# The second block's output product as seven half-size products (Strassen's scheme) instead of eight, with VectorE forming the sums before and after

## What is computed

```python
merged = (jax.nn.sigmoid(g_diff) * (o_diff @ w_proj_diff[layer])
          + jax.nn.sigmoid(g_mla) * (o_mla @ w_proj_mla[layer]))
x = x + merged @ w_out[layer]
...
return rms_norm(x, norm_final)
```

## Time and profile before

| | |
|---|---|
| time, median of 3 | 1087.87 us (1087.51 to 1088.33) |
| the profiled execution: span from its first to its last instruction | 1085.8 us; its time outside the span is not recorded, the median of the timed ones is 2.1 us above it |
| TensorE busy | 1072.4 us (99%) |
| weight loads | 860.1 us (79%) |
| VectorE busy | 712.5 us (66%) |
| ScalarE busy | 420.2 us (39%) |
| mean granted TensorE clock | 0.999 of full speed |

### The profile page before, as it was taken

The page is one execution under the profiler, slowest core; times in us unless marked ns, Lnnn a source line. Parts: engine busy times, 40 slices in busy tenths (PEclk is TensorE's granted clock), DMA queues, the critical chain, the costliest instruction groups (busy, mean ns, idle before and its releaser), DMA issues.

```text
span 1085.8 us, 13595 instructions
## 1 busy us (share of the span) xinstructions
PE 1072.4 (99%) x5395; PEld 860.1 (79%) x5397; DVE 712.5 (66%) x1149; ACT 420.2 (39%) x661; POOL 0.2 (0%) x4
## 2 busy tenths in 40 slices
PE   9999999999999999999999999999999999999998
PEld 6777877977878888888888887887776777888886
DVE  6998877868678887854588745654568446464441
ACT  6513655334443223222222234744367443323232
POOL 0000000000000000000000000000000000000000
PEclk9999999999999999999999999999999999999999
DMA  8422122221213323234322234323121222033302
GB/s 279 126 78 79 47 71 79 71 86 39 79 60 106 117 79 105 59 89 129 122 78 88 65 94 143 98 97 117 44 78 40 78 78 78 1 116 117 102 35 78
DMA packets 100239, 95.59 MB, mean 88 GB/s; under 512 B 5952, under 2 KB 91216, under 8 KB 100176
## 3 DMA queue, kind: packets, MB, share of 16 engines
q1 hardware_dynamic: 100000, 94.71, 27.9%
q10 hardware_dynamic: 176, 0.02, 0.0%
HBM read 92.60 MB, written 2.10 MB: 87 GB/s over the span
## 4 chain that ended last, share of the span: by engine, by line
PE 91%; DVE 5%; ACT 2%; issue 1%; DMA 1%; SPq 0%; DVEq 0%; ACTq 0%
PE ring L1036 22%; PE ring L1038 22%; PE ring L1037 22%; PE bank L1036 3%; PE bank L1038 3%; PE bank L1037 3%; PE bank L1500 1%; PE bank L1295 1%; DVE w_lo L1929 1%; PE bank L1267 1%; DMA w_raw<-in_w_in 1%; PE bank L1200 1%; PE bank L1280 1%; PE bank L1524 1%; PE bank L1473 1%
## 5 line engine op out<-in xcount | busy, mean ns | idle before, releaser
L1036 PE MATMUL ring<-act_hi,w_hi 128*128 128x512 f32 (+2 forms) x808 | 320.2, 396 | 0.9 <-DVE xT L2312 0.5
L1038 PE MATMUL ring<-act_hi,w_lo 128*128 128x512 f32 (+2 forms) x808 | 313.5, 388 | 0.0
L1037 PE MATMUL ring<-act_lo,w_hi 128*128 128x512 f32 (+2 forms) x808 | 313.2, 388 | 0.0
L1588 ACT ACTIVATE w_hi<-w_raw 128x2048 fp32r<-128x2048 f32 (+5 forms) x96 | 159.8, 1665 | 249.7 <-PE ring L1038 200.6
L1929 DVE TENSOR_TENSOR w_lo<-w_raw,w_hi 128x2048 fp32r<-128x2048 f32 (+4 forms) x101 | 190.3, 1886 | 4.2 <-ACT w_hi L1588 3.9
L1036 PEld LDWEIGHTS ring<-act_hi,w_hi 128*128 128x128 f32 x808 | 151.8, 188 | 37.1 <-issue 3.9
L1038 PEld LDWEIGHTS ring<-act_hi,w_lo 128*128 128x128 f32 x808 | 151.7, 188 | 31.6
L1037 PEld LDWEIGHTS ring<-act_lo,w_hi 128*128 128x128 f32 x808 | 151.8, 188 | 31.3 <-issue 1.9
L1036 PE MATMUL ring<-hidH,w_hi 128*128 128x512 f32 x176 | 68.5, 389 | 0.0
L1037 PE MATMUL ring<-hidL,w_hi 128*128 128x512 f32 x176 | 68.5, 389 | 0.0
L1038 PE MATMUL ring<-hidH,w_lo 128*128 128x512 f32 x176 | 68.5, 389 | 0.0
(11 more groups left out here) (363 smaller groups left out, 1618.9 us busy)
## 6 DMA issues: line engine op xcount, KB each, us to landing
w_raw<-in_w_in SPq DMA_DIRECT2D x30, 1024.0 KB, 5.3
w_raw<-in_w_up SPq DMA_DIRECT2D x22, 1024.0 KB, 5.1
w_raw<-in_w_out SPq DMA_DIRECT2D x8, 1024.0 KB, 5.1
w_raw<-in_w_down SPq DMA_DIRECT2D x8, 768.0 KB, 4.7
w_raw<-in_w_down SPq DMA_DIRECT2D x8, 640.0 KB, 4.3
w_raw<-in_w_in SPq DMA_DIRECT2D x7, 512.0 KB, 4.7
xin<-in_xt SPq DMA_DIRECT2D x8, 256.0 KB, 4.1
xT<-in_xt SPq DMA_DIRECT2D x2, 1024.0 KB, 6.6
```

The lines of the kernel that those rows point to most:

```text
L1036: pe.matmul(out, ah, bh, start=(first and n == 0), stop=False)
L1037: pe.matmul(out, ah, bl, start=False, stop=False)
L1038: mm = pe.matmul(out, al, bh, start=False, stop=(last and n == len(pairs) - 1))
L1588: return act.activation(out, src, func, **more)
```

## The change

The 512 x 1024 by 1024 x 1024 product is cut into 2 x 2 quarters: token halves by depth halves on the left, depth halves by column halves on the right (B11, B12, B21, B22, one weight slot each). Eight quarter products become seven, `prod` 0 to 6, each over two blocks of 128 tokens (t = 0, 1). Four of them take a sum on the left (S1 to S4, 128 x 1024), four a sum on the right (T1 to T4, 128 x 2048); these are formed by VectorE in float32 (`s_sum`, `t_sum`) and then split into high and low parts like any operand (`s_split`, `split_form`). `snap`, `s17`, `u_sum`, `v_sum` and `c_sum` put the products together in `xo` in SBUF, with one addition of a bank each (`snap` is a copy by ACT). The residual is opened into products 2, 5 and 6 and, for one quarter, into two tiles of the ring (`res`). Products 1, 3, 4, 5 use T3 with S3, T2 with S2, T1 with S1, B22 with S4; product 6 uses T4 with `mH`. The order of stages is again by hand. `merged` is now kept in float32 (`mt2`, eight slices) for the S sums. B22 and B21 are loaded into the space of the block's input, so only after tile `gm7`. Squares for the norm are taken from `xo` (`sq_early`), scaling of the first finished half rows is `scaled`, of the other `final`. Several semaphores are merged to make room, which moves nothing.

```diff
--- before.py
+++ after.py
+        mt2 = [sb(f"mt2{i}", [P, 4, T], F32, M + (108, 90)[i]) for i in range(2)]
+
+        b22 = sb("b22", [P, SLOT], F32, 64)
+        b21 = sb("b21", [P, SLOT], F32, 72)
+        t1 = sb("t1", [P, SLOT], F32, 80)
+        Sf = {n: sb(f"S{n}f", [P, 4, 256], F32, M + at) for n, at in ((3, 22), (1, 98), (2, 102), (4, 16))}
...
+        B11 = len(chunks)
+        chunk("B11", k_out2[:, 0:4, 0:512])
+        for name in ("T3", "B21", "T2", "T1", "B22", "T4"):
+            form(name)
+        PROD = ("B11", "T3", "B21", "T2", "T1", "B22", "T4")
...
+            if c == 3:
+                stage("s_split", 3)
+                stage("t_sum", "T1")
             for kind in ("pd", "pm"):
                 for i in (2 * c, 2 * c + 1):
+                    if (kind, i) == ("pm", 6):
+                        stage("t_sum", "T3")
                     in_tile(kind, i, f"pj{c}")
+                    if (kind, i) == ("pm", 6):
+                        split_form("T3")
+            if c == 1:
+                stage("s_sum", 3)
+
+        both("prod", 0)
         stage("m_flush")
-        for half in range(2):
-            for part in range(2):
-                chunk(f"w_out2{half}{part}", k_out2[:, 4 * part:4 * part + 4, 512 * half:512 * half + 512])
-            for b in range(NB):
-                stage("out_a", half, b)
-            for b in range(NB):
-                tile(("out", half, b), f"w_out2{half}1")
-                stage("out", half, b)
-                if half == 1:
-                    stage("final", b)
-            last_use[chunk_of[f"w_out2{half}0"]] = tile_at["out", half, 0]
+        split_form("B21")
+        stage("t_sum", "T2")
+        both("snap")
+        both("prod", 1)
+        stage("s_sum", 1)
+        stage("s_sum", 2)
+        split_form("T2")
+        stage("s_split", 2)
+        both("s17")
+        for t in range(2):
+            tile(("res", t))
+            stage("res", t)
+        both("prod", 2)
+        stage("c_sum", 2, 0)
+        stage("s_split", 1)
+        stage("c_sum", 2, 1)
+        split_form("T1")
+        stage("s_sum", 4)
+        each("sq_early", 0, 1)
+        both("prod", 3)
+        split_form("B22")
+        stage("s_split", 4)
+        both("u_sum")
+        both("prod", 4)
+        stage("t_sum", "T4")
+        split_form("T4")
+        both("c_sum", 4)
+        both("v_sum")
+        each("sq_early", 2, 3)
+        both("prod", 5)
+        for t in range(2):
+            stage("scaled", t)
+            stage("c_sum", 5, t)
+        each("final", 0, 1)
+        each("scaled", 2, 3)
+        both("prod", 6)
+        for t in range(2):
+            stage("c_sum", 6, t)
+            stage("final", 2 + t)
...
+            wait_split(sp, B11 - 1)
+            quarter_in(raw[(B11 + 1) % 2], 0, 1, raw_in[(B11 + 1) % 2])
+            sp.wait_ge(tile_done, upto(("gm", KD - 1)))
+            quarter_in(b22, 1, 1, block_in[0])
+            quarter_in(b21, 1, 0, block_in[1])
...
+                elif kind == "prod":
+                    n, t = s[1:]
+                    at = slice(P * t, P * t + P)
...
+                    elif n == 6:
+                        pe.wait_ge(part_sum, 2 * t + 4)
+                    to = bank[2 * (n % 3) + t]
+                    opened = n in RES_OF
+                    if opened:
+                        half, b0 = RES_OF[n]
                         for j in range(4):
...
+                    lh, ll = left_of(n)
+                    wh, wl = weights(PROD[n])
+                    product(to[:], [((lh[:, k, at], ll[:, k, at]), (wh[:, k, :], wl[:, k, :])) for k in range(4)],
+                            first=not opened).then_inc(prod_mm, 1)
...
+                elif kind == "u_sum":
+                    t = s[1]
+                    dve.wait_ge(part_sum, t + 1)
+                    dve.wait_ge(prod_mm, 6 + t + 1)
+                    TT(xo[:, 2 + t, 0:512], xo[:, 2 + t, 512:1024], bank[t][:], ALU.add).then_inc(part_sum, 1)
+                    TT(xo[:, t, 512:1024], xo[:, t, 512:1024], bank[t][:], ALU.add).then_inc(part_sum, 1)
...
+                    TT(xo[:, 2 + t, 512:1024], xo[:, 2 + t, 0:512], at_ring(r)[:], ALU.add).then_inc(bank_free(r), 1)
...
+                elif kind == "c_sum":
+                    n, t = s[1:]
...
+                    TT(to, xo[:, t, 512:1024] if n == 2 else to, bank[2 * (n % 3) + t][:], ALU.add).then_inc(c_sum, 1)
```

More of the change, by code:

```diff
@@ L111, in sem @@
             return ctx.enter_context(nc.semaphore(name))
-        con_in, rest_in, gmix_in, par_in, pos_in, gfin_in = (
-            sem(n) for n in ("con_in", "rest_in", "gmix_in", "par_in", "pos_in", "gfin_in"))
-        x_back_in = [sem(f"x_back_in{i}") for i in range(2)]
+        con_in, rest_in, gmix_in, par_in = (
+            sem(n) for n in ("con_in", "rest_in", "gmix_in", "par_in"))
+        block_in = [sem(f"block_in{i}") for i in range(2)]
         w_hi_done, w_lo_done = (sem(n) for n in ("w_hi_done", "w_lo_done"))
@@ L793, in two_blocks, with split_form, both @@
         attention("mla", 4, "ym", fill)
+        B11 = len(chunks)
[3 more added lines that the diff above has]
+        PROD = ("B11", "T3", "B21", "T2", "T1", "B22", "T4")
+        def split_form(name):
+            stage("w_first", chunk_of[name])
+        def both(kind, *what):
+            for t in range(2):
+                stage(kind, *what, t)
         for c in range(4):
@@ L874, in two_blocks, with left_of, raw_of @@
         assert splits == sorted(splits) == list(range(2, len(chunks))) == [s[1] for s in order if s[0] == "w_lo" and s[-1] != chunks[s[1]][2] // 2]
+        form_raw = {"T3": raw[(B11 + 1) % 2], "B21": b21, "T2": raw[B11 % 2], "T1": t1, "T4": b21, "B22": b22}
+        form_src = {chunk_of[n]: form_raw[n] for n in form_raw}
+        T_SUMS = ("T1", "T3", "T2", "T4")
+        S_SPLITS = (3, 2, 1, 4)
+        kS = B11 % 2
+        SH = {n: sb(f"S{n}H", [P, 4, 256], F32R, at) for n, at in ((3, 88), (2, M + 78), (1, M + 86), (4, 8 * (1 - kS)))}
+        SL = {n: sb(f"S{n}L", [P, 4, 256], F32R, at) for n, at in ((3, 92), (2, M + 82), (1, M + 22), (4, 8 * (1 - kS) + 4))}
+        early_half = (0, 0, 1, 1)
+        S_OF = {1: 3, 3: 2, 4: 1, 5: 4}
+        RES_OF = {2: (0, 0), 5: (1, 0), 6: (0, 256)}
+        ROWS_OF = {2: (0, 0), 4: (2, 1), 5: (0, 1), 6: (2, 0)}
+        def left_of(n):
+            if n in S_OF:
+                return SH[S_OF[n]], SL[S_OF[n]]
+            half, at = {0: (0, 0), 2: (1, 0), 6: (1, 256)}[n]
+            return [m[:, 4 * half:4 * half + 4, at:at + 256] for m in (mH, mL)]
+        EARLY_ROWS, LAST_ROWS = (0, 1, 2, 3), (0, 1, 2, 3)
+        SCALED_ROWS = tuple(s[1] for s in order if s[0] == "scaled")
+        def raw_of(c):
+            return form_src[c] if c in form_src else raw[c % 2]
         landed = []
@@ L909, in two_blocks @@
         EARLY.update({("dv", b): bank[(0, 1, 3, 4)[b]] for b in range(NB)})
-        EARLY.update({("out", half, b): bank[(4 * half + b) % 6] for half in range(2) for b in range(NB)})
         def at_ring(name):
@@ L1542, in _ @@
                     channels(s, f"pj{i // 2}", P * (i % 2), (oH[:, at:at + 4, :], oL[:, at:at + 4, :]), nk=4, part=0 if kind == "pd" else 1)
[L1543 to L1556, removed]
-                        for j in range(4):
[L1558 to L1562, removed]
@@ L1595, in _ @@
                     n = chunks[c][2]
-                    act.wait_ge(raw_in[c % 2], landed[c])
-                    if c >= FIRST:
+                    name = chunks[c][0]
+                    if c <= B11:
+                        act.wait_ge(raw_in[c % 2], landed[c])
+                    elif name in T_SUMS:
+                        act.wait_ge(form_sum, T_SUMS.index(name) + 1)
+                    else:
+                        act.wait_ge(block_in[("B22", "B21").index(name)], 32)
+                    if c >= B11 + FIRST:
+                        act.wait_ge(prod_mm, 2 * (c - B11 - FIRST) + 2)
+                    elif c >= FIRST:
                         act.wait_ge(tile_done, last_use[c - FIRST] + 1)
-                    A(whi[c % 3][:, 0:n], raw[c % 2][:, 0:n], ACT.Identity).then_inc(w_hi_done, 1)
+                    A(whi[c % 3][:, 0:n], raw_of(c)[:, 0:n], ACT.Identity).then_inc(w_hi_done, 1)
                 elif kind == "x":
@@ L1649, in _ @@
                     act.wait_ge(act_step, step())
-                    A(g1[:], g1[:], ACT.Ln, bias=1.0).then_inc(gate_ln, 1)
+                    A(g1[:], g1[:], ACT.Ln, bias=1.0).then_inc(prep_act, 1)
                 elif kind == "decay_in":
```

254 lines of the change are left out of this document (176 added, 78 removed).

## The result

The changed kernel takes 1092.1 us (median of 5, 1091.72 to 1092.64) against 1087.87 (1087.21 to 1088.41): ratio 1.0039, 95% interval 1.0026 to 1.0052. It is 4.2 us slower; forecast was 3.7 us slower, within 1089.6 to 1094.2.

What follows compares the result with a forecast made beforehand. TensorE bounds the kernel before, VectorE's queue the changed one. TensorE saves 5.4 us, loses 2.9 to stalls, and VectorE's late end leaves 3.7 us slower: 1087.87 + 3.7 = 1091.6 us, range 1089.6 to 1094.2 (8 in 10).

Steps and rivals of the forecast that it cites:

- TensorE's saving: Output product: seven quarter products with transposes take 42.0 us against 47.4 before, saving 5.4 us on TensorE.
- First stall: At gm7: VectorE drains pd6 late, so TensorE waits 1.2 us before pm6; charged once.
- the walk: Stepping each engine's new instruction order against traced durations and handovers; it put the last scaling's end at 1086.38, before 1082.69.
- B21's low part: Behind ACT's table load and B21's high part: VectorE idles 2.4 us, B21 ready at 1043.29, TensorE unaffected.
- The long queue: From 1041.01 VectorE never rests: 26.5 us of work, T4 ends at 1067.6, TensorE barely fed.
- T4: T4's high part on ACT, then its low part: VectorE idles 2.1 us, TensorE stalls 1.7 us before product 6.
- The end: Behind T4's low part: VectorE's remaining queue delays product 6's additions; last scaling ends at 1086.38 instead of 1082.69.
- second step: From T3 at 1029.25 through the drains of pm6 and pm7 to B21's low part, ready at 1043.29.
- TensorE bounds: Rival: VectorE keeps up in the queue from 1041 us; last scaling at 1078.0, -4.7, 1083.2 us; 5%.
- A late load: Rival: B22 or B21 lands late, before T3; +0.5 (1092.1) or +2.6 us (1094.2); 9%.
- The clock: Rival: TensorE falls to half rate in a stall; 1095.6 us at pm6 and pm7, 1092.0 at product 6; 7%.
- The tie: No measurable cost, 1085.7 to 1090.0 us: walk too slow by 1.5 us or more, such as shorter handovers; 11%.

Runs made afterwards that it cites:

- e1: The changed kernel with twelve more 128x512 matmuls on TensorE before product 4, result unused; 1091.98 us.
- e2: The changed kernel with two more 128x1024 subtractions on VectorE just before S4, result unused; 1094.86 us.
- e8: The changed kernel's same instructions, with the last 48 steps of VectorE's queue and 24 of ACT's in orders of their own; 1083.57 us.
- e5: The changed kernel with another order at the end: scaled 2 and 3 before final 0, product 6's additions before final 1 and final 2; 1089.86 us.
- e3: The changed kernel with S3's low part and the sum T1 moved behind VectorE's drains of pd6 and pd7; 1094.45 us.
- e7: The changed kernel with three moves together: T4 before S4, the other order at the end, ACT's table load early; 1086.17 us.
- e4: The changed kernel with the sum T4 formed before S4; 1090.07 us.
- e6: The changed kernel with ACT's table load moved from behind the last slice of mH to behind S3's high part; 1090.97 us.
- e9: The changed kernel with the four T sums on GpSimd instead of VectorE; 1094.34 us.
- e11: e8 with two more 128x1024 subtractions on VectorE just before T4; 1086.25 us.

## Why the prediction was right

The mechanism was right, and not only the time: VectorE's queue, with its waits for ACT, ends last, and TensorE's saving goes unused (e1 and e2). **TensorE's saving**: 42.0 us of products forecast, 42.1 measured (from product 0's first matmul at 1034.88 to 1078.99, less the wait of 2.0), with no wait between products 0 and 5. **First stall**: 1.2 forecast, 1.1 measured. In the walk it holds pm6's drain back by 0.2 us behind T3's end; in the trace the two fall together, so nearly all of it is covered. **B21's low part**: VectorE idle 2.4 forecast, 2.54 measured. **The long queue**: from B21's low part to T4's start 24.3 us both forecast (1041.01 to 1065.31) and measured (1042.02 to 1066.31). **T4**: idle 2.1 forecast, 1.99 measured; second stall 1.7 forecast, 2.0 measured. **The end**: product 6's additions 6.2 and 5.7 us behind their banks forecast, 6.1 and 5.6 measured.

**What was mis-sized.** The stretch came out at 64.64, not 64.04. Nearly all of the 0.6 us lies in two handovers of the second step. T3 starts 0.34 us late against the walk (shifted by gm7's 0.49), since each drain of pd6 and pd7 is followed by a wait for itself before the bank is given free: they cost 0.83 and 0.73 us in the queue instead of 0.61 each. Of this 0.27 is left at pm7's drain. The rest is the table load, which neither begins before the slice of mH ends nor lets the next activation begin early:

```profile
1038.12 0.63 ACT L1704 ACTIVATE mH<-mt 128x512 fp32r<-128x512 f32 x1 [3.29 <-DVEq L2701]
1038.78 1.28 ACT L2014 ACT_TABLE_LOAD   x1
1040.07 1.92 ACT L1704 ACTIVATE w_hi<-b 128x2048 fp32r<-128x2048 f32 x1
```

So B21's low part is 0.5 us late, and from there on the walk is off by 0.50 to 0.60.

**The rivals.** TensorE bounds: refuted by e1 and e2 for the changed kernel, and true of e8. A late load: the two loads landed 5.2 and 7.6 us after issue, and T3 waited only for VectorE's queue. The clock: whole in the changed kernel's trace up to the last product, but half at the same place in e5's, and in e2's and e3's behind waits of 3.2 and 2.3 us (windows of 1075 to 1080 at 0.50 and 0.66). The prediction's sign of being wrong, a clock below 1 in the last 60 us, is met to the letter, at 0.50 from 1082 us on, but only when TensorE has no work left, and costs nothing. Half the clock in product 6 was put at 0.4 us; e2, e3 and e5 show none of it in the stretch (67.15, 66.83 and 61.93 against 67.1, 66.9 and 61.9 expected). At the first stall the clock never fell in these traces, so the 4.0 us put on it there is not tested; whether it falls behind the second one differs between traces of the same wait, and what decides that stays open. The tie: what it needed was not shorter handovers but another order (e7, e8).

## What to carry to other kernels

Fewer products on the engine that bounds pay only if the engine that forms and merges the sums has its queue laid out as carefully: count its added work against the stretch that is left, then walk both queues in order. In this queue, which took on 35 us more within some 60, the waits for ACT that were taken away (2.0 us in e4, 1.4 in e6) came back in full at the end. A stall of the former bottleneck need not be a loss: taking one away by putting VectorE's work later cost 2.2 us here, while 1.4 us of VectorE's idle time taken away at a place where TensorE never waited gave back 1.4. Lay sums a few steps ahead of the copy that needs them, put table loads where the engine idles, and drain a finished bank before anything that waits for a chain through another engine.

## What the runs showed of the hardware

- A GpSimd sum of 128x2048 takes 4.6 to 5.5 us where VectorE's takes 2.28, and holds off VectorE instructions with two SBUF operands that come up during it until its end (0.69 us becomes 5.00), but not those with one operand in PSUM (two in 1.51 us), nor one that had started before it (1.22 us) (e9).
- A table load of ACT took 1.28 us and overlapped with neither of its neighbours: the activation before it ended at 1038.75, the load ran from 1038.78, the next activation from 1040.07 (the changed kernel).
- After a wait of TensorE of 2.0 us the clock fell to half in one trace (e5: eight matmuls 0.43 us apart) and stayed whole in another (the changed kernel). It also fell behind waits of 2.3 (e3), 3.2 (e2) and 3.8 us (e9), and stayed whole behind one of 2.2 (e11).
- An in-order walk with durations from the trace before, mended at two places by the trace after, forecast the stretch of ten further runs (56 to 67 us) to 0.2 us or better, and their times to 0.6. The one miss is e9, for whose GpSimd sums no row existed.
